# Scale row and biases of the experts made during the output product, their sum begun in the first expert, the router by halves of the tokens

## The chip, the cores and the metric

The kernel runs on one core of one Trainium2 chip. The metric is the device time of one execution in microseconds (us), the median of several runs. Times inside an execution are counted from the start of its span. Engine names are those of the profile: PE is the matrix engine (PEld its weight loads, PEq its sequencer), DVE the vector engine, ACT the scalar engine, POOL the GpSimd engine, SP the engine that issues most DMAs. A matmul in full float32 leaves two records in the trace, a transpose one.

## The reference, cut to what matters

The program is two blocks over 256 tokens of width 1024. The first has attention with an output product and then a mixture of 32 experts, of which each token uses 4; the second has an mLSTM layer and an attention layer with their dense feed-forward parts. The change lies where the first block goes from attention to the experts:

```
x = x + g_a * _merge(ya, yb, ga, gb, w_oa, w_ob, w_out)      # output product
hx = _modulate(_rmsnorm(x, norm_mlp), sh_m, sc_m)
logits = (h @ router_w + router_b).astype(jnp.float32)
top_logit, top_e = lax.top_k(logits, TOP_K)
top_w = jax.nn.softmax(top_logit, axis=-1)
...
gate = jnp.minimum(xe @ w_gate[e] + b_gate[e], SWIGLU_LIMIT)
up = jnp.clip(xe @ w_up[e] + b_up[e], -SWIGLU_LIMIT, SWIGLU_LIMIT)
act = (up + 1) * (gate * jax.nn.sigmoid(SWIGLU_ALPHA * gate))
return act @ w_down[e] + b_down[e]
...
x = x + g_m * moe(hx)
```

## The kernel before, in words

The five engines have programs of their own, written out by hand, which wait on semaphores; nothing reorders them. The 256 tokens are two halves q of 128 rows, the 1024 columns two halves h of 512.

*Output product.* Steps t = 42 to 49 each take one slice of 128 rows of `w_out`. ACT and DVE split each slice into a high and a low float32r part (`high_a`, `low_a`), and PE runs three matmuls per product (`mm3`, L625 to L627). Steps 42 to 45 run inside the loop over t; the last four slices run quarter by quarter (q, h), L876 to L888, so that the rows of one quarter are finished while PE is at the next. ACT works for step t + 4 in the pass of step t, in order.

*Norm and router.* `next_norm("a")` on DVE and ACT adds each quarter to X (two DVE operations), squares it (ACT, L1561), takes the root (ACT, L1566) and makes a diagonal matrix of the inverse. `turn_rows_a(q)` on PE (L805 to L812) multiplies X by it, which turns and scales 128 columns k at a time into PSUM banks 0 to 3; ACT evicts the even k (L1574), DVE the odd (L1861) into `b.h2`. `turn_rows_a(0)` runs before the last quarter of the product, `turn_rows_a(1)` after it. Then PE makes the router's logits for both halves (L381), spreads the row g_m over 128 partitions (8 matmuls, L900, banks 0 and 1), turns `b.h2` back to token rows (16 transposes, L909), turns the picks (L913, L915) and the places (L918, L919), and begins the experts' sum with weights times scaled down-biases (4 matmuls into the banks `b.Y`, L926). ACT, after its last eviction, loads the table of Exp (L1594), copies the spread row twice per half (`b.gm`, `b.gm2`), issues the four DMAs of the gate and up biases (`b.brow`, L1602), then computes the router's exponential for q = 0 (L1611), evicts turned tokens (`rows_to_gather`), the exponential for q = 1 and the rest. DVE does the router's steps for q = 0 and 1 (L2130 to L2142), scales the down-biases (`bdn`, L2145), counts the tokens of each expert (L2148 and on) and writes a flag.

*Experts.* Every engine loads the flag into a register and branches; with these inputs the branch for few tokens per expert is taken. For each expert PE gathers its tokens (L941, by the selection that DVE makes in `select`), turns them (L952), adds the biases (L985) and runs the gate and up products in two parts, k0 = 0 and k0 = 4 (L990, 32 records each). A part's end frees two of six slots of weights, each of 2 MB. In the middle come `put_back` of the expert before (L960, not in expert 0), `turn_act(ex, 0)`, the gather for the next expert and `turn_act(ex, 1)`, then the down product in two parts (L1023), each of which frees one slot. SP issues the loads in one fixed order and waits for the freed slot before each (L605); the first expert's six slots are loaded before the router.

## Time and profile before

| | |
|---|---|
| median of 3 runs | 1972.54 us (1970.38 to 1973.79) |
| profiled execution | 1973.61 us |
| its span | 1971.6 us, so 2.0 us lie around it |
| mean granted clock of PE | 0.972 of full |
| PE busy | 93% of the span |
| DMA, mean | 286 GB/s |

The profile's page names the costliest groups and the chain of work that ended last. The change touches some 60 us of the span between the end of the output product and the first expert, so the views that matter here are the chain, the timeline and the queue of SP in that stretch. PEclk is the share of the full clock of 2.4 GHz that PE was granted: 0.50 is 1.2 GHz.

### The profile page before, as it was taken

Reading aid. Unit: us, or ns where it says so; the run is one execution under the profiler, and the core shown is the slowest. Engines: PE = TensorE matmul, PEld = TensorE weight load, DVE = VectorE, ACT = ScalarE, POOL = GpSimd, SP = SyncE. Lnnn points to the kernel's source line nnn. Section 1 sums busy time; section 2 is a strip of 40 time slices with the busy share of each in tenths; the row PEclk is TensorE's granted clock in tenths of the full one; section 3 lists DMA queues with packets and bytes.
Section 4 is the critical chain, followed back from the end, with each engine's and each line's share of the span. In section 5 each row is a group of like instructions: output and inputs, shape, how many; then the busy total and the mean of one; then the engine's idle time right before and its main releaser. Section 6 shows DMA issues by size and latency. Waiting matters only on the chain.

```text
span 1971.6 us, 24815 instructions
## 1 busy us (share of the span) xinstructions
PE 1828.4 (93%) x10349; PEld 1126.6 (57%) x10349; DVE 772.6 (39%) x1348; ACT 601.0 (30%) x1076; POOL 19.5 (1%) x59
## 2 busy tenths in 40 slices
PE   5999988899999999999999999979999999899999
PEld 4987757233333333333333333348789997778998
DVE  2665534323222223223222222144555455645554
ACT  3456543111110111111110111145554445555442
POOL 0100010000000000000000000000000000000000
PEclk9999988899999999999999999989999999999999
DMA  8523764499999999999999999965326454324550
GB/s 294 195 74 124 258 258 175 187 427 429 426 427 428 428 427 428 428 426 429 426 429 426 429 426 428 427 225 207 122 95 212 171 202 161 128 86 159 184 178 36
DMA packets 122050, 563.27 MB, mean 286 GB/s; under 512 B 7216, under 2 KB 53424, under 8 KB 97360
## 3 DMA queue, kind: packets, MB, share of 16 engines
q1 hardware_dynamic: 120912, 558.44, 70.8%
q10 hardware_dynamic: 1024, 3.22, 0.4%
q8 instruction: 84, 1.38, 0.3%
q14 instruction: 30, 0.25, 0.0%
HBM read 560.58 MB, written 1.05 MB: 285 GB/s over the span
## 4 chain that ended last, share of the span: by engine, by line
PE 63%; DMA 29%; DVE 3%; ACT 2%; issue 1%; SPq 0%; ACTq 0%; DVEq 0%
DMA ring<-in_w_up 27%; PE ps L990 15%; PE ps L625 12%; PE ps L626 12%; PE ps L627 12%; PE ps L1023 3%; DMA ring<-in_w_ada 2%; PE ps L637 1%; PE ps L1114 1%; DVE part L1864 1%; PE ps L732 1%; PE ps L941 1%; ACT part L1347 1%; PE ps L960 1%; PE ps L742 1%
## 5 line engine op out<-in xcount | busy, mean ns | idle before, releaser
L625 PE MATMUL ps<-part,part 128*128 128x256 f32 (+2 forms) x1592 | 512.9, 322 | 10.9 <-DVE part L1864 8.6
L990 PE MATMUL ps<-ring,arena 128*64 128x512 f32 x2048 | 463.1, 606 | 46.1 <-DMA ring<-in_w_up 46.0
L626 PE MATMUL ps<-part,part 128*128 128x256 f32 (+2 forms) x1592 | 504.5, 317 | 0.0
L627 PE MATMUL ps<-part,part 128*128 128x256 f32 (+2 forms) x1592 | 503.8, 316 | 0.0
L1864 DVE TENSOR_TENSOR part<-ring,part 128x1024 fp32r<-128x1024 f32 (+1 forms) x299 | 313.2, 1090 | 136.9 <-ACT part L1347 136.3
L990 PEld LDWEIGHTS ps<-ring,arena 128*64 128x64 f32 x2048 | 157.5, 139 | 349.5 <-issue 349.5
L625 PEld LDWEIGHTS ps<-part,part 128*128 128x128 f32 (+1 forms) x1592 | 306.7, 193 | 42.4 <-issue 16.0
L627 PEld LDWEIGHTS ps<-part,part 128*128 128x128 f32 (+1 forms) x1592 | 306.0, 192 | 19.8
L626 PEld LDWEIGHTS ps<-part,part 128*128 128x128 f32 (+1 forms) x1592 | 306.8, 193 | 17.6
L1347 ACT ACTIVATE part<-ring 128x1024 fp32r<-128x1024 f32 (+1 forms) x299 | 271.8, 947 | 29.3 <-PE ps L627 24.1
L1861 DVE TENSOR_SCALAR arena<-ps 64x512 f32<-64x512 f32 x128 | 88.1, 688 | 400.4 <-PE ps L990 394.7
L1023 PE MATMUL ps<-ring,arena 128*64 128x512 f32 x1024 | 233.6, 598 | 0.0
L1657 ACT ACTIVATE arena<-arena 64x512 f32<-64x512 f32 x64 | 40.3, 630 | 633.8 <-DVE arena L1861 633.8
L1347 ACT ACTIVATE arena<-ps 128x256 f32<-128x256 f32 (+3 forms) x192 | 84.0, 476 | 240.1 <-PE ps L952 117.5
L1864 DVE TENSOR_TENSOR arena<-ps,arena 128x512 f32<-128x512 f32 x40 | 27.4, 686 | 302.5 <-PE ps L1023 295.8
L1023 PEld LDWEIGHTS ps<-ring,arena 128*64 128x64 f32 x1024 | 67.9, 136 | 117.6 <-issue 115.4
L1864 DVE TENSOR_TENSOR ring<-ps,ring 128x256 f32<-128x256 f32 (+1 forms) x52 | 23.8, 464 | 146.3 <-ACT ring L1771 145.8
L1771 ACT ACTIVATE ring<-ps 128x256 f32<-128x256 f32 x44 | 16.9, 384 | 185.4 <-PE ps L627 185.4
L1864 DVE TENSOR_TENSOR arena<-arena 64x512 f32<-64x512 f32 (+2 forms) x68 | 70.0, 1029 | 2.4
L1347 ACT ACTIVATE ring<-ps 128x512 f32<-128x512 f32 (+2 forms) x87 | 43.2, 518 | 72.6 <-PE ps L627 17.3
L960 PE MATMUL ps<-arena 64*128 64x512 f32 x256 | 63.6, 615 | 0.8 <-DVE arena L1864 0.8
L941 PE MATMUL ps<-arena 128*64 128x512 f32 x256 | 63.2, 615 | 0.0
(245 smaller groups left out, 1009.0 us busy)
## 6 DMA issues: line engine op xcount, KB each, us to landing
ring<-in_w_gate SPq DMA_DIRECT2D x64, 2048.0 KB, 16.8
ring<-in_w_up SPq DMA_DIRECT2D x64, 2048.0 KB, 21.4
ring<-in_w_down SPq DMA_DIRECT2D x64, 2048.0 KB, 19.0
ring<-in_ffn_w_in SPq DMA_DIRECT2D x44, 1024.0 KB, 7.8
ring<-in_w_ada SPq DMA_DIRECT2D x12, 2048.0 KB, 11.2
ring<-in_ffn_w_out SPq DMA_DIRECT2D x10, 2048.0 KB, 8.0
ring<-in_w_in SPq DMA_DIRECT2D x8, 2048.0 KB, 11.6
ring<-in_a_w_in SPq DMA_DIRECT2D x6, 2048.0 KB, 10.8
```

The lines of the kernel that those rows point to most:

```text
L625: e.matmul(out, x[0], y[0], start=first, stop=False, skip_group_check=True)
L626: e.matmul(out, x[0], y[1], start=False, stop=False, skip_group_check=True)
L627: return e.matmul(out, x[1], y[0], start=False, stop=last, skip_group_check=True)
L637: i = e.matmul(PS[bank][32 * g:32 * g + 32, :], a.c32[:, g + 4 * r, :], w[:, g + 4 * r, :], start=r == 0, stop=r == 1, skip_group_check=True)
L941: i = e.matmul(PS[p][CAP * h:CAP * h + CAP, :], S[:, CAP * q:CAP * q + CAP], b.htok[:, q, 512 * h:512 * h + 512], start=q == 0, stop=q == ...
L960: i = e.matmul(b.Y[q][h], b.PwT[ex % 2][CAP * h:CAP * h + CAP, 128 * q:128 * q + 128], b.yg[ex % 2][CAP * h:CAP * h + CAP, :], start=False ...
L990: i = e.matmul(PS[p + h][CAP * r:CAP * r + CAP, :], xg[:, k0 + k, :], W(("moe_" + "gu"[r], ex, k0))[:, k, 512 * h:512 * h + 512], start=False,
L1023: i = e.matmul(PS[p + 1][CAP * h:CAP * h + CAP, :], aT[:, k0 + k, :], W(w)[:, k, 512 * h:512 * h + 512], start=k0 == 0 and k == 0, stop=k0 ...
L1347: return e.activation(out, src, ACT.Copy)
L1657: e.activation(gus[:, 2, 512 * h:512 * h + 512], gus[:, 0, 512 * h:512 * h + 512], ACT.Sigmoid, scale=1.702).then_inc(*s_sig.up(ex, h))
L1861: return e.tensor_scalar(out, x, s1, s2, op0, op1) if op1 is not None else e.tensor_scalar(out, x, s1, None, op0)
L1864: return e.tensor_tensor(out, x, y, op)
```

## The change

Six edits, all in the stretch above:

1. The spread of g_m on PE moves from behind the logits to step t = 44 of the output product, into banks 2 and 3; ACT's four copies of it move to the same step, between `high_a(48)` and `high_a(49)`. PE waits for the last copy before the first of the four quarters.
2. DVE's two scalings of `bdn` move ahead of `next_norm("a")`.
3. The four DMAs of `b.brow` move from ACT to SP, behind the load of slab `gb1`, with a wait for the last heads' norm (`s_kn.of(9)`).
4. The logits of q = 0 are made between the product's end and `turn_rows_a(1)`, those of q = 1 after it.
5. ACT evicts all eight turned pieces of q = 1; DVE evicts none of them and can go on to the router of q = 0.
6. The four matmuls that begin the sum move into expert 0, behind its gate and up products (and to the head of the other branch, which does not run here).

`b.gm`, `b.gm2`, `b.xtok` and `b.brow` get other places in memory, since they are now written earlier.

```diff
@@ sync_program
+                if key == ("in", "gb1"):
+                    e.wait_ge(*s_kn.of(9))
+                    for r, n in enumerate(("b_gate", "b_up")):
+                        for h in range(2):
+                            at = 32 * (2 * r + h)
+                            e.dma_start(b.brow[at:at + 32, :], A[n][0][:, 512 * h:512 * h + 512]).then_inc(*s_brow.up(r, h))
@@ tensor_program
-                        e.wait_ge(*(s_ulo if i % 2 else s_uhi).of("moe", i - 4))
+                        e.wait_ge(*(s_ulo if i % 2 and i < 12 else s_uhi).of("moe", i - 4))
...
+                if t == 44:
+                    e.wait_ge(*s_mod.of(11))
+                    for h in range(2):
+                        for j in range(4):
+                            i = e.matmul(PS[2 + h][:, 128 * j:128 * j + 128], M(5, 4 * h + j).to_broadcast([128, 128]), C("ident"),
+                                         start=True, stop=True, skip_group_check=True)
+                        i.then_inc(*s_gm.up(h))
+            e.wait_ge(*s_gm2.of("half", 1))
...
-            turn_rows_a(1)
-            e.wait_ge(*s_small_ld.of("biases"))
-            e.wait_ge(*s_uhi.of("moe", 14))
-            e.wait_ge(*s_ulo.of("moe", 15))
-            for q in range(2):
+            def logits(q):
                 mm(e, PS[4 + q][:, 0:NE], [(b.h2[:, k, 128 * q:128 * q + 128], rw[:, k, :]) for k in range(KT)]
                    ).then_inc(*s_logit.up(q))
-            for h in range(2):
-                for j in range(4):
-                    i = e.matmul(PS[h][:, 128 * j:128 * j + 128], M(5, 4 * h + j).to_broadcast([128, 128]), C("ident"),
-                                 start=True, stop=True, skip_group_check=True)
-                i.then_inc(*s_gm.up(h))
+            e.wait_ge(*s_small_ld.of("biases"))
+            e.wait_ge(*s_uhi.of("moe", 6))
+            e.wait_ge(*s_ulo.of("moe", 7))
+            logits(0)
+            turn_rows_a(1)
+            e.wait_ge(*s_uhi.of("moe", 15))
+            logits(1)
...
                     if ex:
                         put_back(ex - 1)
+                    else:
+                        begin_sum()
                     turn_act(ex, 0)
@@ scalar_program
+                if t == 44:
+                    for h in range(2):
+                        e.wait_ge(*s_gm.of(h))
+                        copy(b.gm[:, 512 * h:512 * h + 512], PS[2 + h]).then_inc(*s_gm2.up(h))
+                        copy(b.gm2[64 * h:64 * h + 64, :], PS[2 + h][64 * h:64 * h + 64, :]).then_inc(*s_gm2.up("half", h))
...
-                    if stage == "a" and i % 2:
+                    if stage == "a" and q == 0 and i % 2:
@@ vector_program
-                    if stage == "a" and i % 2 == 0:
+                    if stage == "a" and (q or i % 2 == 0):
...
+            for h in range(2):
+                e.wait_ge(*s_gm2.of(h))
+                tt(bdn[:, 512 * h:512 * h + 512], bdn[:, 512 * h:512 * h + 512], b.gm[0:NE, 512 * h:512 * h + 512], ALU.mult
+                   ).then_inc(*s_bdn.up(h))
             next_norm("a")
```

`begin_sum` is the removed loop of L921 to L927 as a function, with the same waits and no signal.

PE from the last matmul of the product (L627, in the changed kernel L632) to the first gather (L941, now L954), before; L811 is `turn_rows_a(1)`, L381 the logits, L900 the spread, L909 the transposes of `b.h2`, L926 the begun sum:

```order
L811 MATMUL ps<-arena,X 128x128 [waits u_high,diag_ready]
...
L381 MATMUL ps<-rw,arena 128x32 [waits u_low,u_high,small_tables_loaded]
L381 MATMUL ps<-rw,arena 128x32 x15
L900 MATMUL ps<-con,mod 128x128 x8
L909 MATMUL ps<-con,arena 128x128 x8
...
L926 MATMUL ps<-bdn,arena 128x512 [waits h_turn_evicted,down_bias_scaled,picks_evicted]
L926 MATMUL ps<-bdn,arena 128x512 x3
L934 TENSOR_LOAD arena [waits places_evicted,bias_rows_loaded,flag_ready]
```

and in the changed kernel (L816 is `turn_rows_a(1)`, L918 the transposes of `b.h2`):

```order
L381 MATMUL ps<-rw,arena 128x32 [waits u_low,u_high,small_tables_loaded]
L381 MATMUL ps<-rw,arena 128x32 x7
L816 MATMUL ps<-arena,X 128x128 [waits u_high,diag_ready]
...
L816 MATMUL ps<-arena,X 128x128 [waits u_high] x4
L381 MATMUL ps<-rw,arena 128x32 [waits u_high]
L381 MATMUL ps<-rw,arena 128x32 x7
L918 MATMUL ps<-con,arena 128x128 x16
...
L947 TENSOR_LOAD arena [waits h_turn_evicted,places_evicted,bias_rows_loaded,flag_ready]
```

Half of the logits went ahead of the turning, the spread and the begun sum are gone from between the turning and the load of the flag (L934, now L947).

ACT behind its last squares of the norm, before; L1574 evicts turned pieces, L1347 is every copy, L1611 the exponential:

```order
L1574 ACTIVATE arena<-ps,mod,small 128x128 [waits u_turned] x4
L1594 ACT_TABLE_LOAD
L1347 ACTIVATE arena<-ps 128x512 [waits gain_row_spread]
L1347 ACTIVATE arena<-ps 64x512
L1347 ACTIVATE arena<-ps 128x512 [waits gain_row_spread]
L1347 ACTIVATE arena<-ps 64x512
L1602 DMA arena<-in_b_gate 32x512 x2
L1602 DMA arena<-in_b_up 32x512 x2
L1611 ACTIVATE small<-small 128x32 [waits router_steps]
```

and now, with L1595, L1363 and L1623 for the same:

```order
L1595 ACTIVATE arena<-ps,mod,small 128x128 [waits u_turned] x8
L1615 ACT_TABLE_LOAD
L1623 ACTIVATE small<-small 128x32 [waits router_steps]
L1363 ACTIVATE arena<-ps 128x512 [waits h_turned] x2
L1623 ACTIVATE small<-small 128x32 [waits router_steps]
```

Four copies and four DMA issues no longer stand before the first exponential, and four more evictions stand before the table load.

PE in expert 0 of the changed kernel: L1003 is the gate and up products, L937 the begun sum, L985 `turn_act`, L954 the gather for expert 1:

```order
L1003 MATMUL ps<-ring,arena 64x512 [waits slot5_loaded,slot3_loaded]
L1003 MATMUL ps<-ring,arena 64x512 x15
L937 MATMUL ps<-bdn,arena 128x512 [waits h_turn_evicted,down_bias_scaled,picks_evicted]
L937 MATMUL ps<-bdn,arena 128x512 x3
L985 MATMUL ps<-con,arena 128x64 [waits expert_act]
```

The begun sum now stands behind both parts of the gate and up products and ahead of all that follows.

## Rows read from the trace of the kernel before

**Rows 1.** Page, the chain that ended last: shares of the span by line.
```profile
DMA ring<-in_w_up 27%; PE ps L990 15%; PE ps L625 12%; PE ps L626 12%; PE ps L627 12%; PE ps L1023 3%; DMA ring<-in_w_ada 2%; PE ps L637 1%; PE ps L1114 1%; DVE part L1864 1%; PE ps L732 1%; PE ps L941 1%; ACT part L1347 1%; PE ps L960 1%; PE ps L742 1%
```
**Rows 2.** Window of 50 us: PE, PEld, DVE, ACT, POOL busy, PEclk, DMA share, GB/s.
```profile
414.00:464.00 50.00, 49.07 (x240) 16.79 (x238) 15.36 (x26) 5.50 (x11) 0.00 (x0) 1.00 1.00 426
```
**Rows 3.** Chain in order of time, 290 to 400 us: start, us, what.
```profile
303.09 0.87 PE ps L802 x8
...
324.26 0.24 PE ps L627
...
327.79 3.80 PE ps L811 x16
...
332.17 7.00 PE ps L381 x32
339.18 3.59 PE ps L900 x16
...
351.30 7.01 PE ps L926 x8
358.31 3.11 PE ps L941 x8
...
364.52 13.91 PE ps L990 x64
```
**Rows 4.** Queue of SP in order of time: start, us, what, loads.
```profile
191.02 0.58 SPq L605 DMA_DIRECT2D ring<-in_w_in  x1
204.80 0.37 SPq L605 DMA_DIRECT2D ring<-in_w_ada  x1
...
371.58 0.33 SPq L605 DMA_DIRECT2D ring<-in_w_gate  x1
...
398.05 0.33 SPq L605 DMA_DIRECT2D ring<-in_w_gate  x1
```
**Rows 5.** Windows of 1 us, same columns: the granted clock.
```profile
326.00:327.00 1.00, 0.00 (x0) 0.00 (x0) 0.16 (x1) 0.77 (x3) 0.00 (x0) 0.80 0.00 0
...
343.00:344.00 1.00, 1.00 (x8) 1.00 (x7) 0.00 (x0) 0.98 (x2) 0.00 (x0) 0.67 0.24 47
...
360.00:361.00 1.00, 1.00 (x6) 0.24 (x2) 0.00 (x0) 0.00 (x0) 0.00 (x0) 0.64 0.00 0
```
**Rows 6.** Timeline: start, us, engine, line, operation, [idle before, releaser].
```profile
307.89 1.23 DVE L1864 TENSOR_TENSOR part<-ring,part 128x1024 fp32r<-128x1024 f32 x1 [0.60 <-ACT part L1347]
...
328.63 0.46 ACT L1574 ACTIVATE arena<-ps,mod,small 128x128 f32<-128x128 f32 x1 [1.41 <-PE ps L811]
...
331.66 1.28 ACT L1594 ACT_TABLE_LOAD   x1
...
335.87 0.19 DVE L1864 TENSOR_TENSOR small<-ps,rb 128x32 f32<-128x32 f32 x1 [3.84 <-PE ps L381]
...
344.60 0.32 ACT L1611 ACTIVATE small<-small 128x32 f32<-128x32 f32 x1 [0.60 <-issue]
...
345.44 0.59 ACT L1347 ACTIVATE arena<-ps 128x512 f32<-128x512 f32 x1
345.62 0.18 DVE L1864 TENSOR_TENSOR small<-ps,rb 128x32 f32<-128x32 f32 x1
...
347.55 0.19 DVE L2140 SCALAR_TENSOR_TENSOR small<-small 128x32 f32<-128x32 f32 x1
```
**Rows 7.** Timeline from the picks to the first selection, same columns.
```profile
348.60 0.42 ACT L1347 ACTIVATE arena<-ps 32x128 f32<-32x128 f32 x2 [0.76 <-PE ps L915]
349.34 0.67 DVE L2148 TENSOR_TENSOR_SCAN arena<-arena 32x256 f32<-32x256 f32 x1
...
353.09 1.77 DVE L1861 TENSOR_SCALAR arena<-con,small 128x64 f32<-128x64 f32 x8 [1.05 <-issue]
```
**Rows 8.** Timeline of DVE behind the end of the experts' branch, same columns.
```profile
1307.13 0.23 DVE L1864 TENSOR_TENSOR part<-wgt,part 128x64 fp32r<-128x64 f32 x1 [4.85 <-issue]
```
**Rows 9.** Line L934, PE's load of the flag: ns min/median/max, first and last start us.
```profile
L934 PEldq TENSOR_LOAD <-arena x1: 492/492/492, 352.1 to 352.1; - x1
```

More of the change, by code:

```diff
@@ L403, in build @@
         b.yg, b.PwT = [alloc(512) for _ in range(2)], [alloc(T) for _ in range(2)]
-        b.S, b.xtok = [alloc(6 * CAP) for _ in range(2)], alloc(512)
-        assert at[0] >= mark + 10 * T + 4 * 512
-        b.gm, b.gm2 = alloc(D), alloc(512)
+        b.S = [alloc(6 * CAP) for _ in range(2)]
+        at[0] = mark + 10 * T + 4 * 512
         b.h3 = at[1][:, at[0]:at[0] + KT * T].rearrange("p (k n) -> p k n", k=KT)
         b.gus = [alloc3(3, D, CAP) for _ in range(2)]
+        b.brow = alloc(512)
         at[0] = mark
@@ L905, in tensor_program @@
                     n = 2 * q + g
-                    if q:
-                        e.wait_ge(*s_gm2.of("half", g))
                     for j in range(4):
@@ L1029, in tensor_program @@
             with e.Else():
+                begin_sum()
                 for n in range(4):
@@ L1594, in scalar_program @@
             e.preload_act_table(ACT.Exp)
-            for h in range(2):
-                e.wait_ge(*s_gm.of(h))
-                copy(b.gm[:, 512 * h:512 * h + 512], PS[h]).then_inc(*s_gm2.up(h))
-                copy(b.gm2[64 * h:64 * h + 64, :], PS[h][64 * h:64 * h + 64, :]).then_inc(*s_gm2.up("half", h))
-            for r, n in enumerate(("b_gate", "b_up")):
-                for h in range(2):
-                    at = 32 * (2 * r + h)
-                    e.dma_start(b.brow[at:at + 32, :], A[n][0][:, 512 * h:512 * h + 512]).then_inc(*s_brow.up(r, h))
             def rows_to_gather(n):
@@ L2116, in next_norm @@
                     turned_low(i)
+            e.wait_ge(*s_small_ld.of("biases"))
+            for h in range(2):
+                e.wait_ge(*s_gm2.of(h))
+                tt(bdn[:, 512 * h:512 * h + 512], bdn[:, 512 * h:512 * h + 512], b.gm[0:NE, 512 * h:512 * h + 512], ALU.mult
+                   ).then_inc(*s_bdn.up(h))
             next_norm("a")
-            e.wait_ge(*s_small_ld.of("biases"))
             def step(i, *key):
@@ L2142, in vector_program @@
                 ts(E, E, s[:, 3:4], None, ALU.mult).then_inc(*s_pick.up("W", q))
-            for h in range(2):
-                e.wait_ge(*s_gm2.of(h))
-                tt(bdn[:, 512 * h:512 * h + 512], bdn[:, 512 * h:512 * h + 512], b.gm[0:NE, 512 * h:512 * h + 512], ALU.mult
-                   ).then_inc(*s_bdn.up(h))
             e.wait_ge(*s_pickTe.of(1))
```

24 lines of the change are left out of this document (12 added, 12 removed).

## The prediction

> **What bounds the kernel now.** I read the chain that ended last first. Its largest single part is a transfer, the up weights of the experts, with 27% of the span [rows 1]: for most of the experts the chain runs through the weight stream, not through PE. The windows say the same: inside the expert loop the DMA share is 1.00 at 426 GB/s [rows 2]. So the question for any change ahead of the experts is when that stream starts. The queue of SP answers: the first load that needs a freed slot is issued at 371.58 [rows 4], when the first half of the first expert's gate and up products is done. Six loads of 2048 KB per expert are 12.6 MB, 29.5 us at 426 GB/s, and everything behind follows the start of this stream, as long as it never runs dry.
>
> Then I read the chain in order of time up to there. After the last product at 324.50 PE waits for the norm until 327.79, turns the second half (3.80), makes the logits (7.00), spreads the row (3.59), and after a stretch of small steps on DVE and ACT begins the sum (7.01), gathers (3.11) and starts the gate and up products at about 364.5 [rows 3]. The one-microsecond windows give the clock: it falls to 0.50, that is 1.2 GHz, during 326 to 327, with PE idle since 324.50; it comes back during 343, falls again before the begun sum, and comes back during 360 [rows 5]. So logits, spread, begun sum and most of the gather run at half speed. On ACT the first exponential starts at 344.60 [rows 6], though the logits of q = 0 were read by DVE at 335.87 [rows 6]: ACT stood behind the spread, its copies and four DMA issues.
>
> **The change part by part**, on the time axis of the profiled execution.
>
> *Spread at t = 44.* Eight matmuls are 16 records. At the full clock 8 records of this width take 0.87 [rows 3], so 16 take 1.75, where PE is saturated: the end of the product moves from 324.50 to 326.25. ACT's four copies take 0.6 each [rows 6], 2.4 in all; the first two lie beside the second half of the spread, and PE has another step of the product (12 matmuls of some 0.23, 2.7) before it waits for the last copy, so that wait is nothing. The last slice's split on DVE ended at 309.12 before [rows 6]; it now comes behind the copies, about 3 later, at 312.2, and PE reads it in the fourth product of the first quarter, near 313. That cover is 0.7; if it is gone the cost is what is missing. DVE's two scalings of the biases (0.6 each) fit between that and the first quarter's end, near 313.6. If all of this were late the whole chain would move by up to 1.
>
> *Bias rows on SP.* Behind `gb1`, issued at 191.02, SP has nothing to do until 204.80 [rows 4]: 13 us for four issues of 64 KB. The event it waits for belongs to a step long past. Cost 0; if the issues took longer than that gap, the load behind them would be late by the rest, and I allow 1.
>
> *Logits of q = 0.* They fall into the wait for the norm, 326.25 to 329.54 (both ends of the old wait, moved by 1.75). At full clock they take a quarter of the 7.00 [rows 3], 1.75; at half clock 3.5, which would push the turning by 0.2. Cost 0.
>
> *Turning and evicting q = 1.* First eviction at 328.63 [rows 6] + 1.75 = 330.38. PE at half clock gives a piece each 0.43 (ACT's fourth, the seventh piece, ended by the table load at 331.66 and so began by 331.2, six pieces behind 328.63), and an eviction on ACT takes 0.46 [rows 6], so the last ends at 330.38 + 3.0 + 0.46 = 333.85. ACT alone keeps up with PE at half clock. The table load of 1.28 [rows 6] follows, to 335.2, and the exponential of q = 0 to 335.5: it needs only DVE's steps, which began at 329.8.
>
> *Logits of q = 1.* Half clock: 3.50, 333.95 to 337.45; DVE reads them 0.2 later, 337.65.
>
> *Transposes of `b.h2`* at half clock, 0.22 a record as in the spread (3.59 / 16) [rows 3]: four groups end at 338.35, 339.25, 340.15, 341.05. ACT copies two groups (0.6 each), to 340.0, then does the exponential of q = 1 (0.32), 340.3. DVE's steps between the read of the logits and the sum took 345.62 to 347.55 [rows 6], 1.93, so DVE is there at 339.6 and waits 0.75 for ACT; from the sum to the weights 0.7, so 341.1. ACT meanwhile copies the other two groups, to 341.8, and the picks (2 x 0.42 [rows 7]), to 342.65. DVE's count starts at 342.75; before it started at 349.34 [rows 7], behind the scaling of the biases that is now gone from there.
>
> *To the first gather.* From that count to the end of the first selection: 349.34 to 353.09 plus half of 1.77 [rows 7], 4.63. The gather could start at 347.4. PE no longer has the begun sum (7.01) in front of it, but now waits out the selection. Before it started at 358.31 [rows 3]. Saved: 358.31 - 347.45 = 10.9.
>
> *The load of the flag on PE.* Before it began at 352.1 and took 0.49 [rows 9], hidden by the begun sum; now nothing hides it. DVE needs 1.05 for its own flag and branch [rows 7], and the selection comes on top of that, so I take 0 for PE, and the other end is the 4.85 that DVE idles behind the branch's end [rows 8]: then PE is ready at 345.3 + 4.85 = 350.2 and the start is 2.7 later. The Trainium skill, "Runtime: NRT & Kernel Launch", section "Instruction fetch mechanics", says that a taken branch to a target outside the prefetched window costs an instruction fetch. The row at the branch's end looks like it, the 1.05 at its entry does not. By that rule, were PE's entry such a branch, the sum would be 2.7 smaller.
>
> *Clock at the gather.* Before, the clock came back during 360, 2.4 us into the gather [rows 5]. Now PE has been nearly idle from 341.4 to 347.4, so it starts at 1.2 GHz again, with no begun sum ahead of it. I take 2 us more at half clock than before, 1.0 lost. The ends: 0, and 5.8 (the first rival below).
>
> *Begun sum in expert 0.* At full clock half of 7.01, 3.5, on PE between two parts of the same expert. It stands behind the release of 371.58. The next start of an expert's loads was at 398.05, the stream of the expert before it lasts to 371.58 + 29.5 = 401.1, both plus the same latency: a slack of 3.0. So 0.5 would come through; but the small steps behind it on PE wait for DVE and ACT, which run on beside it, and I expect that to give the half back. PE's round from release to release is 26.5 and the stream's 29.5, so the slack is whole again an expert later. Cost 0, other end 3.5.
>
> **Sum.** Stream start and all behind it: -10.9 + 1.0 = -9.9. The profiled execution took 1973.61, of which 1971.6 are its span, so 1963.7. The median of the runs shown is 1.07 lower, 1972.54, and the forecast for a median is 1962.6.
>
> **Rivals** (for a median).
>
> *The clock comes back late.* With neither a long transposing stretch nor the begun sum ahead, the half clock may last through the gather and the first half of the gate and up products. From 326.6 to 343.7 it lasted 17 us although PE was busy [rows 3, 5]; the second time it was back 9.4 us after the begun sum's start at 351.30. 14 us from the gather's start, against 2.4 before, lose (14 - 2.4) / 2 = 5.8 in place of 1.0: 1967.4. The chance is 20%.
>
> *The clock never falls in the router.* The logits of q = 0 fill more than half of the idle stretch in which it fell. Then logits and transposes take half: the last eviction ends at 333.3, the logits of q = 1 at 335.2, and ACT's chain ends with the picks at 339.3, so the gather starts at 344.0 and 14.3 are saved, 13.3 with the loss at the gather: 1959.2. Against it: the remaining gap of 1.5 us and thin work around it. 9%.
>
> *The begun sum starves the stream.* If PE is slower in expert 0 than I take, the slack of 3.0 is used up and up to 3.5 come back: 1966.1. The margin is nothing by my own sum. 13%.
>
> *PE's branch*, as above, 2.7 back: 1965.3. 4%.
>
> *Slower: the half clock holds through the whole first expert and into the second.* Every us of it costs 0.5 on PE once it decides. 45 us from the gather's start lose 22.5 - 1.2 for what was there before, less the slack of 3.0, 18.3, against 10.9 saved: +7.4, 1979.9. It turns slower where the half clock lasts more than about 30 us. Against it: the clock came back within the gather [rows 5], and the first expert's 64 records took 13.91, the full rate [rows 3]. 4%.
>
> **How the numbers follow.** The forecast as worked out has 50%. 1962.6 is its time. The cases reach from 1959.2 to 1967.4 and the executions before differed by some 3 us, so the range is 1957.5 to 1968. A difference under 0.2%, 3.9 us, can't be told from no change with this kernel. Faster by more than that means under 1968.6: the forecast, and nearly all of the other cases but the last, 0.90. Within 0.2%: the upper end of the late clock, 0.06. Slower: 0.04.
>
> **What would show it right or wrong.** Right: the last product near 326.3; logits in two groups of about 1.8 and 3.5; first exponential near 335; gather near 347.4; begun sum of some 3.5 in eight records behind the first expert's gate and up products; the first gate load of the second expert near 361.7, that of the third about 26.5 to 29.5 later with no gap in the DMA share. Wrong: a stream start later than 365, DMA share under 0.95 in the 30 us behind it, a PE wait between the spread and the first quarter, a clock of 0.50 under the gate and up products, or a weight load of the first block that is later than before behind the bias rows. The forecast fails most easily in the clock: two of its terms assume which level is granted.

## The result and the profile after

The changed kernel takes 1958.13 us (median of 4 runs, 1955.34 to 1960.53), against 1972.69 for the kernel before beside it: ratio 0.9925, 95% interval 0.9912 to 0.9937. The forecast was 1962.6, faster. The profiled execution took 1958.61, its span is 1956.8 and its mean granted clock 0.979. The nine runs of this kernel in two series (the second in the experiments below) have a median of 1958.61 and reach from 1955.34 to 1963.69.

Line numbers have moved: the product is now L630 to L632, the spread L885, the turning L816, the transposes L918, the picks L922 and L924, the gather L954, gate and up L1003, the begun sum L937, SP's loads L604. On the page the chain still has the up weights as its largest part [rows 1]:

```profile
DMA ring<-in_w_up 28%; PE ps L1003 14%; PE ps L630 12%; PE ps L631 12%; PE ps L632 12%; PE ps L1038 3%; DMA ring<-in_w_ada 2%; PE ps L642 1%; DVE part L1876 1%; PE ps L1130 1%; PE ps L954 1%; PE ps L737 1%; ACT part L1363 1%; PE ps L747 1%; PE ps L973 0%
```

The queue of SP shows both the gain and a loss (start, us, what, loads; answers to [rows 4]):

```profile
190.02 0.58 SPq L604 DMA_DIRECT2D ring<-in_w_in  x1
190.65 3.75 SPq L610 DMA_DIRECT2D arena<-in_b_gate  x2
194.44 0.89 SPq L610 DMA_DIRECT2D arena<-in_b_up  x2
203.80 0.38 SPq L604 DMA_DIRECT2D ring<-in_w_ada  x1
...
356.49 0.33 SPq L604 DMA_DIRECT2D ring<-in_w_gate  x1
...
388.86 0.33 SPq L604 DMA_DIRECT2D ring<-in_w_gate  x1
```

The stream of weights starts at 356.49, where it was 371.58: 15.09 earlier. But the next expert's loads start 32.37 later, not 26.47. One expert's weights last 29.5 by the prediction's estimate (29.36 from start to start where the stream bounds the loop), so the queues ran empty for some 2.9. The bias rows took 4.7 us of SP and the load behind them is 13.8 behind `gb1`'s, as before: they cost nothing. The load of `gb1` itself is 1.0 earlier than before, ahead of anything that the change touches: executions differ by that much before the change begins.

The chain in order of time (start, us, what; answers to [rows 3]):

```profile
305.35 1.78 PE ps L885 x16
...
324.89 0.24 PE ps L632
...
328.95 3.38 ACT arena L1595 x8
332.35 1.28 ACT L1615
333.64 0.33 ACT small L1623
...
337.65 0.43 ACT arena L1363 x2
338.11 0.69 DVE arena L2160
...
342.86 3.47 PE ps L954 x8
...
349.43 13.88 PE ps L1003 x64
363.31 4.03 PE ps L937 x8
367.96 3.61 PE ps L954 x8
```

The spread is in the chain with 1.78. ACT's evictions, the table load and the exponential of q = 0 follow each other without a gap, and behind the first expert's products now stands the begun sum. PE's own timeline (start, us, engine, line, operation, idle before, releaser) has what is off this chain:

```profile
324.96 1.86 PE L381 MATMUL ps<-rw,arena 128*128 128x32 f32 x16
328.43 3.41 PE L816 MATMUL ps<-arena,X 128*128 128x128 f32 x16 [1.60 <-DVE arena L1873]
332.38 1.97 PE L381 MATMUL ps<-rw,arena 128*128 128x32 f32 x16 [0.55 <-ACT arena L1595]
334.19 1.94 PE L918 MATMUL ps<-con,arena 128*128 128x128 f32 x16
```

The logits come in two groups, each 1.9 long; the transposes take 1.94. All three ran at the full clock, but the turning between them (3.41) didn't. The one-microsecond windows say when it was granted, the five-microsecond one what the DMA did behind the begun sum (start:end, length, PE, PEld, DVE, ACT, POOL busy, PEclk, DMA share, GB/s; answer to [rows 2, 5]):

```profile
328.00:329.00 1.00, 0.57 (x4) 0.57 (x5) 0.90 (x8) 0.05 (x1) 0.00 (x0) 0.93 0.00 0
332.00:333.00 1.00, 0.62 (x6) 0.62 (x6) 0.00 (x0) 0.98 (x2) 0.00 (x0) 0.86 0.00 0
...
345.00:346.00 1.00, 1.00 (x4) 0.00 (x0) 0.00 (x0) 0.00 (x0) 0.00 (x0) 0.54 0.00 0
366.00:367.00 1.00, 1.00 (x3) 0.11 (x1) 0.56 (x1) 0.00 (x0) 0.00 (x0) 0.70 1.07 459
373.00:374.00 1.00, 1.00 (x6) 0.29 (x6) 0.00 (x0) 0.23 (x1) 0.00 (x0) 0.88 1.11 475
381.00:386.00 5.00, 5.00 (x28) 1.49 (x22) 1.36 (x5) 0.00 (x0) 0.00 (x0) 1.00 0.91 338
```

The half clock lasts from 329 to 332 only, under the turning; then from 339 to 346 with the gather in it; and a third time from 366 to 373, from the end of the begun sum on. Before, it lasted from 326 to 343 and from 350 to 360, and none fell behind the first expert. From 381 the DMA moves 338 GB/s, where it is near 426 inside the loop [rows 2]: the dry stretch.

**The account.** The span is 14.8 shorter: -15.1 up to the stream's start, +2.65 between it and the last expert's second gate and up part (910.36 before, 913.01 now), -0.9 from there to the next block's turning and -1.5 behind that. The change doesn't touch the last two. From that part of the last expert to the end of the span the fourteen profiles take between 685.2 and 689.7, with the same work there; the kernel before is the longest of them (689.66, the changed one 687.30). The starts of that part on PE's timeline, before and after, show one piece of it:

```profile
1281.94 8.79 PE L990 MATMUL ps<-ring,arena 128*64 128x512 f32 x32 [2.38 <-DMA ring<-in_w_up]
```

```profile
1269.50 7.09 PE L1003 MATMUL ps<-ring,arena 128*64 128x512 f32 x32 [1.69 <-DMA ring<-in_w_up]
```

Before, the clock was at 0.50 from 1282 to 1286, and the same 32 records took 1.7 longer.

### The profile page after: what moved, and what is told of

Read it like the earlier page. It is cut to its first block, busy times and chain, and to the rows that moved or that the text cites. A ratio compares the mean times of both kernels' runs of the same rounds, so it can differ in the third digit from the quotient of the medians.

```text
span 1956.8 us, 24817 instructions
## 1 busy us (share of the span) xinstructions
PE 1814.3 (93%) x10349; PEld 1117.3 (57%) x10349; DVE 770.5 (39%) x1344; ACT 602.0 (31%) x1080; POOL 19.5 (1%) x59
## 4 chain that ended last, share of the span: by engine, by line
PE 62%; DMA 30%; DVE 3%; ACT 3%; issue 2%; SPq 0%; DVEq 0%; ACTq 0%
DMA ring<-in_w_up 28%; PE ps L1003 14%; PE ps L630 12%; PE ps L631 12%; PE ps L632 12%; PE ps L1038 3%; DMA ring<-in_w_ada 2%; PE ps L642 1%; DVE part L1876 1%; PE ps L1130 1%; PE ps L954 1%; PE ps L737 1%; ACT part L1363 1%; PE ps L747 1%; PE ps L973 0%
## 5 line engine op out<-in xcount | busy, mean ns | idle before, releaser
L630 PE MATMUL ps<-part,part 128*128 128x256 f32 (+2 forms) x1592 | 512.5, 322 | 10.9 <-DVE part L1876 8.6
L632 PE MATMUL ps<-part,part 128*128 128x256 f32 (+2 forms) x1592 | 503.4, 316 | 0.0
L1003 PE MATMUL ps<-ring,arena 128*64 128x512 f32 x2048 | 457.7, 600 | 46.4 <-DMA ring<-in_w_up 46.3
L1003 PEld LDWEIGHTS ps<-ring,arena 128*64 128x64 f32 x2048 | 156.1, 138 | 345.9 <-issue 345.9
L630 PEld LDWEIGHTS ps<-part,part 128*128 128x128 f32 (+1 forms) x1592 | 306.2, 192 | 42.4 <-issue 16.0
L632 PEld LDWEIGHTS ps<-part,part 128*128 128x128 f32 (+1 forms) x1592 | 305.7, 192 | 19.8
L1363 ACT ACTIVATE part<-ring 128x1024 fp32r<-128x1024 f32 (+1 forms) x299 | 271.8, 947 | 27.7 <-PE ps L632 22.1
L1363 ACT ACTIVATE arena<-ps 128x256 f32<-128x256 f32 (+3 forms) x192 | 84.0, 477 | 234.3 <-PE ps L965 117.7
L954 PE MATMUL ps<-arena 128*64 128x512 f32 x256 | 65.2, 632 | 2.8 <-DVE arena L1873 2.8
L1363 ACT ACTIVATE ring<-ps 128x512 f32<-128x512 f32 (+2 forms) x87 | 43.2, 518 | 71.9 <-PE ps L632 17.3
```

What stands on the lines that cost most here:

```text
L630: e.matmul(out, x[0], y[0], start=first, stop=False, skip_group_check=True)
L632: return e.matmul(out, x[1], y[0], start=False, stop=last, skip_group_check=True)
L954: i = e.matmul(PS[p][CAP * h:CAP * h + CAP, :], S[:, CAP * q:CAP * q + CAP], b.htok[:, q, 512 * h:512 * h + 512], start=q == 0, stop=q == ...
L1003: i = e.matmul(PS[p + h][CAP * r:CAP * r + CAP, :], xg[:, k0 + k, :], W(("moe_" + "gu"[r], ex, k0))[:, k, 512 * h:512 * h + 512], start=False,
L1363: return e.activation(out, src, ACT.Copy)
```

## The experiments

For each kernel I read the same moments. F is the end of the output product (read from PE's timeline, 0.15 below the chain's reading), G the start of the first gather, S the start of the stream (SP's first gate load for a freed slot), S2 that of the next expert, E the start of the last expert's second gate and up part.

| kernel | median us | ratio, 95% | F | G-F | S-G | S2-S | E-S |
|---|---|---|---|---|---|---|---|
| before | 1972.7 | 1 | 324.3 | 33.90 | 13.34 | 26.47 | 910.36 |
| changed | 1958.1 | 0.9925 [0.9912, 0.9937] | 325.0 | 17.89 | 13.63 | 32.37 | 913.01 |
| e0 changed, again | 1959.9 | 0.9944 [0.9930, 0.9957] | 326.0 | 18.00 | 14.02 | 30.93 | 911.20 |
| e1 sum before flag | 1962.4 | 0.9953 [0.9939, 0.9967] | 326.5 | 22.42 | 13.81 | 26.47 | 910.43 |
| e2 sum late | 1959.6 | 0.9939 [0.9925, 0.9952] | 324.7 | 18.09 | 13.92 | 26.47 | 910.41 |
| e3 only sum moved | 1970.5 | 0.9989 [0.9980, 0.9998] | 325.6 | 29.75 | 13.86 | 32.37 | 913.03 |
| e4 logits together | 1966.2 | 0.9964 [0.9950, 0.9978] | 325.1 | 24.42 | 14.19 | 30.88 | 911.15 |
| e5 spread behind logits | 1964.5 | 0.9956 [0.9939, 0.9972] | 325.0 | 22.91 | 13.74 | 32.38 | 913.06 |
| e6 bias rows on ACT | 1958.9 | 0.9936 [0.9919, 0.9952] | 326.0 | 18.06 | 13.95 | 30.94 | 911.49 |
| e7 dense filler | 1958.8 | 0.9935 [0.9920, 0.9950] | 325.1 | 17.96 | 13.55 | 29.30 | 910.90 |
| e8 evictions shared | 1960.6 | 0.9935 [0.9919, 0.9952] | 325.7 | 16.72 | 15.86 | 30.94 | 911.67 |
| e9 three together | 1958.6 | 0.9932 [0.9919, 0.9946] | 327.3 | 20.31 | 14.15 | 26.48 | 910.17 |
| e10 clock kept up | 1959.3 | 0.9935 [0.9922, 0.9949] | 328.7 | 22.64 | 12.13 | 26.48 | 910.29 |
| e11 filler cut | 1955.9 | 0.9910 [0.9894, 0.9927] | 325.8 | 17.90 | 12.12 | 26.48 | 910.31 |

The moments are from one profiled execution each, which need not be near the median: that of e4 is the fastest of its five, those of e9 and e10 the slowest of theirs. F alone varies by 4. The medians are of 4 to 11 runs and tell kernels apart from about 3 us upwards.

**e0_changed_again.** The changed kernel, unchanged.

> The changed kernel unaltered, timed beside the others on the same chip. Both theories: ratio to before 0.9925, between 0.991 and 0.994. Its profile tells in how many executions the clock falls under the begun sum.

Same G-F as in the first profile (18.00, 17.89), but 1.8 less between S and E. What differs there is the clock: at half for 3.4 behind the begun sum, for 6.8 in the first profile. More on it in e7.

**e1_sum_before_flag.** The begun sum back to its old place, all else as changed.

```diff
+            begin_sum()
             e.wait_ge(*s_flag.of())
...
-                    else:
-                        begin_sum()
```

> The changed kernel with the begun sum back ahead of the load of the flag. Theory A (the begun sum in expert 0 lets the weight stream run dry for 2.7 us and took 4.2 us from before the gather): the gather comes 4.2 us later than in the changed kernel, the stream has no gap, so 1.5 us slower than the changed kernel. Rival B (in expert 0 it costs nothing): 4.2 us slower.

```profile
342.00 7.03 PE L937 MATMUL ps<-bdn,arena 32*128 32x512 f32 x8
348.96 3.62 PE L955 MATMUL ps<-arena 128*64 128x512 f32 x8
```

On PE's timeline the sum runs at half clock, 7.03, and the gather stands right behind it: G-F is 4.4 longer, and nothing is dry any more (S2-S 26.47). So by the profiles moving the sum was worth some 2 to 4: it takes 4.4 off the path in front and returns 0.8 (e0) to 2.6 (first profile) behind. The medians differ by 2.5, which they can't tell from nothing by themselves; they don't contradict it.

**e2_sum_late.** The begun sum in experts 8 to 11, one matmul each; expert 0's `put_back` starts the banks.

```diff
-                                         b.yg[ex % 2][CAP * h:CAP * h + CAP, :], start=False, stop=ex == NE - 1,
+                                         b.yg[ex % 2][CAP * h:CAP * h + CAP, :], start=ex == 0, stop=ex == NE - 1,
...
+                    if 8 <= ex < 12:
+                        q, h = (ex - 8) // 2, (ex - 8) % 2
+                        e.matmul(b.Y[q][h], b.wT[:, 128 * q:128 * q + 128], bdn[:, 512 * h:512 * h + 512], start=False, stop=False,
+                                 skip_group_check=True)
```

> The changed kernel without any begun sum: the put-back of expert 0 starts the sum, and the four matmuls of weights times down-biases are added one each in experts 8 to 11, where PE waits 1.7 us for weights. Theory A: the stream has no gap, 2.7 us faster than the changed kernel. Rival B: the same time as the changed kernel, within 0.5 us.

```profile
356.69 0.33 SPq L604 DMA_DIRECT2D ring<-in_w_gate  x1
...
383.16 0.33 SPq L604 DMA_DIRECT2D ring<-in_w_gate  x1
```

SP's queue shows 26.47 between the two, and E-S is 910.41, the figure of before. The stream is never dry, and all the extra of the changed kernel between S and E is the begun sum. The medians (1959.6 and e0's 1959.9) can't tell the two apart, as against a profiled gain of 0.8 to 2.6.

**e3_only_sum_moved.** The kernel before with edit 6 alone, the same lines as in e1 the other way.

> The kernel before with the begun sum alone moved into expert 0. Theory A: the gather starts when the first selection is done, 4.2 us earlier than before, and the stream runs dry by up to 2.7 us: 1.5 to 4.2 us faster than before. Rival B: 4.2 us faster, no gap in the stream. Rival C (the clock comes back later without the begun sum ahead of the gather): no gain or up to 2 us slower than before.

G-F falls by 4.15, and 2.67 come back as a dry stream, which leaves 1.5. The measured gain is 2.2 (0.9989, 0.9980 to 0.9998): theory A. In the kernel before only 4.15 of the sum's 7.01 lay on the path, since the count and the selection ran beside it.

**e4_logits_together.** Both halves' logits behind the turning again; all else as changed.

```diff
-            logits(0)
             turn_rows_a(1)
             e.wait_ge(*s_uhi.of("moe", 15))
+            logits(0)
             logits(1)
```

> The changed kernel with the logits of both halves made behind the turning, none in the wait for the norm. From the product's end to the first gather the changed kernel takes 17.9 us. Theory C (the logits of q = 0 in that wait keep PE at 2.4 GHz through the turning): here the clock falls in the wait, turning and logits run at 1.2 GHz, and the stretch takes 22 us or more. Rival D (the clock is luck, the logits do not hold it): the clock under the turning is as in the changed kernel, and only the router's steps of q = 0 move behind the logits: 20.2 us.

```profile
328.71 3.75 PE L816 MATMUL ps<-arena,X 128*128 128x128 f32 x16 [3.51 <-DVE arena L1873]
333.01 7.04 PE L381 MATMUL ps<-rw,arena 128*128 128x32 f32 x32 [0.55 <-ACT arena L1595]
339.86 3.65 PE L918 MATMUL ps<-con,arena 128*128 128x128 f32 x16
```

PE idles 3.51 ahead of the turning, the clock falls in that wait and stays at half until 344: logits 7.04, transposes 3.65. G-F is 6.5 longer, the median 6 to 8. Moving 1.9 us of work can't do that by its own length. The clock adds 3.2 to the two groups of logits and 1.7 to the transposes; with the 1.9 that is 6.8, against 6.5 in G-F. The three profiles without logits in that wait (before, e3, e4) have the clock fall there, at 326 to 328, and stay at half for 17. In none of the eleven with them did it fall in that wait, of which 1.6 are left.

**e5_spread_behind_logits.** Edits 1 and 2 undone: the spread, its copies and the scalings where they were.

```diff
-                if t == 44:
...
             logits(1)
+            for h in range(2):
+                for j in range(4):
+                    i = e.matmul(PS[h][:, 128 * j:128 * j + 128], M(5, 4 * h + j).to_broadcast([128, 128]), C("ident"),
+                                 start=True, stop=True, skip_group_check=True)
...
```

> The changed kernel with the spread of the scale row, its copies and the scaling of the down-biases back behind the logits. The product ends 1.8 us earlier. Theory A': the first exponential waits for spread (1.8 to 3.6) and four copies, and the scaling (1.2) stands before the count again: the stretch to the gather takes 22 to 25 us, and the kernel is 2.5 to 5 us slower than the changed one. Rival B' (ACT and DVE had room there): the stretch stays under 20 us and the kernel is within 0.5 us of the changed one.

```profile
331.91 1.97 PE L381 MATMUL ps<-rw,arena 128*128 128x32 f32 x16 [0.91 <-ACT arena L1589]
333.71 3.41 PE L908 MATMUL ps<-con,mod 128*128 128x128 f32 x16
```

G-F is 4.9 longer: the spread at mostly half clock (3.41), and ACT's copies ahead of its first exponential, against the spread inside the product, which makes that longer by 2.0: from the turning behind step 43 (303.56 in e5, 301.58 in the changed kernel) to F it takes 21.4 here and in the other two kernels without the spread there, 23.4 with it. F is no earlier than in the changed kernel only because this execution was 2.0 behind already at 303.56. So edits 1 and 2 are worth 2.9 in the profiles. The median is 4.6 to 6.4 longer.

**e6_bias_rows_on_act.** Edit 3 undone: ACT issues the four DMAs, behind its table load.

```diff
             e.preload_act_table(ACT.Exp)
+            for r, n in enumerate(("b_gate", "b_up")):
+                for h in range(2):
+                    at = 32 * (2 * r + h)
+                    e.dma_start(b.brow[at:at + 32, :], A[n][0][:, 512 * h:512 * h + 512]).then_inc(*s_brow.up(r, h))
```

> The changed kernel with the four DMAs of the bias rows issued by ACT again, behind its table load. Theory A': four issues of 0.44 us stand before the first exponential, which comes 1.8 us later; the stretch to the gather grows by 1.4 us. Rival B': issues run beside ACT's work, since the exponential is not what ends the wait; the stretch stays at 17.9 us, within 0.3.

```profile
332.91 1.28 ACT L1609 ACT_TABLE_LOAD   x1
332.92 0.92 ACTq L1613 DMA_DIRECT2D arena<-in_b_up  x2
334.20 0.32 ACT L1621 ACTIVATE small<-small 128x32 f32<-128x32 f32 x1
```

The issues run on ACT's queue beside its last evictions and the table load, and the exponential follows the table at once. The edit is worth nothing that shows: G-F 18.06, median 1958.9 against 1959.9 and 1958.1.

**e7_dense_filler.** As e2, and in expert 0, where the begun sum stood, four matmuls of 128 rows whose result is overwritten: extra work.

```diff
+                    else:
+                        for q in range(2):
+                            for h in range(2):
+                                e.matmul(b.Y[q][h], b.htok[:, 0, 128 * q:128 * q + 128], b.htok[:, 1, 512 * h:512 * h + 512], start=True,
+                                         stop=False, skip_group_check=True)
```

> The begun sum is made late, in experts 8 to 11, as in e2_sum_late; in its place in expert 0 stand four dense matmuls (128 rows by 512 columns, full float32, 8 records) into the same banks, whose result is overwritten. They are extra work and change no output. In the changed kernel the clock fell to 0.50 while the begun sum, whose matmuls have 32 rows, ran in the first expert, and the stream of weights ran dry by 2.7. Theory F: the clock fell because the 32-row matmuls are thin; with 128 rows in the same place it stays near full, the filler takes 1.8 to 2.2 for 8 records, and the next expert's loads start 28 to 30 behind the first's: no gap in the stream, median within 1 of e2_sum_late. Rival F': the clock falls at this place whatever the matmuls are (the pause behind the first expert's products is its cause): the filler takes 3.4 to 4.0, the loads are 31 to 32.4 apart, the stream is dry for 1.5 to 2.9, median 1.5 to 3 above e2_sum_late.

PE's timeline first of e0, then of e7:

```profile
364.80 3.70 PE L937 MATMUL ps<-bdn,arena 32*128 32x512 f32 x8
368.82 3.31 PE L954 MATMUL ps<-arena 128*64 128x512 f32 x8
```

```profile
363.37 3.70 PE L1032 MATMUL ps<-arena 128*128 128x512 f32 x8
...
367.39 1.94 PE L954 MATMUL ps<-arena 128*64 128x512 f32 x8
```

Both groups of 8 records take 3.70. Behind the 32-row ones the gather of the next expert takes 3.31, behind the 128-row ones 1.94: there the clock stayed at 1.00 throughout, S2-S is 29.30 and E-S 910.90. The begun sum stands in expert 0 in seven profiles, and in every one the clock falls during it or within 1 us of its end: for 3.4 us in e0, e4, e6 and e8 (S2-S near 30.9), for 6.8 in the changed kernel, e3 and e5 (32.4). In e1, e2, e7, e9, e10 and e11 it does not fall there. So theory F holds as far as one filler in one profile can show. My figure for 8 records at full clock, 1.8 to 2.2, was wrong by my own rows: they are 3.5 to 3.7. Priced by E-S: the length alone 0.5, with 3.4 us of half clock 0.8 to 1.3, with 6.8 us 2.65. The four kernels with S2-S near 30.9 differ by 0.5 themselves, so the first figure is no more than that scatter.

**e8_evictions_shared.** Edit 5 undone: DVE evicts the odd pieces of q = 1 again.

```diff
-                    if stage == "a" and q == 0 and i % 2:
+                    if stage == "a" and i % 2:
...
-                    if stage == "a" and (q or i % 2 == 0):
+                    if stage == "a" and i % 2 == 0:
```

> The changed kernel with the evictions of q = 1 shared by ACT and DVE again. Theory E (with the clock at 2.4 GHz PE gives a piece each 0.22 us and ACT's 0.42 per eviction is what bounds the turning): the last eviction comes 1.5 to 2 us earlier, and the stretch to the gather takes about 1.2 us less than in the changed kernel. Rival F (DVE's router steps of q = 0, now late, cost as much as is won): the same or up to 1 us more.

```profile
329.17 2.19 PE L816 MATMUL ps<-arena,X 128*128 128x128 f32 x16 [1.60 <-DVE arena L1874]
...
342.44 3.68 PE L955 MATMUL ps<-arena 128*64 128x512 f32 x8 [2.78 <-DVE arena L1874]
...
348.62 1.98 PE L999 MATMUL ps<-arena,con 32*64 32x512 f32 x8 [0.69 <-ACT arena L1364]
```

The gather comes 1.2 sooner behind F, for at full clock PE's turning takes 2.19 where it doesn't wait for ACT, and eight evictions on ACT alone take 2.90 (e0; 3.38 in the first profile, where the turning was at half clock). But here the half clock lasted from 338 to 351 (the biases took 1.98 in place of 1.09) and S-G is 2.2 longer. From F to S it is 32.6, against 31.5 in the first profile and 32.0 in e0: no gain. Whether edit 5 costs anything in the median stays open.

**e9_three_together.** e2 and e8 together, and the table of Exp loaded while ACT waits for the turning.

```diff
                 root_of(1)
+                if stage == "a":
+                    e.preload_act_table(ACT.Exp)
                 for i in range(8, 16):
...
-            e.preload_act_table(ACT.Exp)
```

> Three things at once on the changed kernel: the begun sum is spread over experts 8 to 11 (as e2_sum_late), DVE takes its share of the evictions of q = 1 again (as e8_evictions_shared), and ACT loads the table of Exp between its second root and these evictions, where it waits 1.1 for PE, not behind them. Expected by adding up: the stream is not dry (-2.7 in the profile), the last product to the first gather is 16.7 as in e8, and the exponential of q = 0 comes 1.28 earlier. Theory H: the path to the gather goes through the logits and the router of q = 1 by then, so the earlier table gives at most 0.4: gather 16.3 to 16.7 behind the last product, stream start 13.9 to 15.9 behind the gather by the clock; profiled span 1953 to 1956, median 1956 to 1958.5. Rival H': the path still goes through ACT's exponential of q = 0: the gather comes 1 to 1.3 earlier still, 15.4 to 15.7. A second rival: the table load takes the wait of 1.1 and 0.2 more, the first evictions are late and nothing is gained: 16.9 or more.

No number for the gather held in the profile: G-F was 20.31. On PE's timeline the clock had fallen already at 321, in the wait ahead of the product's last quarter, was back from 326 to 332, and was at half again to 342:

```profile
323.70 0.77 PE L630 MATMUL ps<-part,part 128*128 128x512 f32 x1
...
334.61 3.59 PE L381 MATMUL ps<-rw,arena 128*128 128x32 f32 x16 [0.59 <-DVE arena L1880]
338.01 3.65 PE L919 MATMUL ps<-con,arena 128*128 128x128 f32 x16
```

Up to the wait for the turning this kernel's work on every engine is e8's, so the fall at 321 is the clock's course in one execution, and not the edits. The median of five runs is 1958.6, just above what the parts sum up to. The early table shows no gain here or in e11, whose G-F is that of the changed kernel. But in both the clock was at half under the turning, and in e8 it wasn't, so what it is worth stays open; it was not tried alone.

**e10_clock_kept_up.** As e9, with dense matmuls into a free bank where PE waits for the gather: extra work.

```diff
+            def keep_busy(m):
+                for j in range(m):
+                    e.matmul(PS[5], b.h2[:, j, 0:128], b.h2[:, 2 * (j % 4):2 * (j % 4) + 2, :], start=True, stop=True,
+            keep_busy(3)
             e.wait_ge(*s_pick.of("pos"))
...
+            keep_busy(2)
...
             e.wait_ge(*s_flag.of())
...
+                keep_busy(3)
                 gather(0)
```

> As e9_three_together, with eight dense matmuls (128 rows by 512 columns, 0.43 each at full clock) into a free bank where PE waits before the first gather: three before the places are turned, two before the flag's load, three between it and the gather. They are extra work and change no output. Theory G: the clock is at half when the gather starts because PE idles in front of it; with the filler it stays at 1.00 from 337 on, the gather takes 1.8 to 2.2 in place of 3.5 to 3.7, and the stream starts 12 to 12.6 behind the gather in place of 13.6 to 15.9: span and median 1 to 2.5 below e9_three_together. Rival G': the filler does not reach (its stretches are broken by the waits) and delays the turned places or the flag by 0.4 to 1.3 each: stream start as late as in e9_three_together or up to 2 later.

```profile
346.38 0.31 PE L934 MATMUL ps<-con,arena 32*128 32x32 f32 x2
...
346.65 4.73 PE L928 MATMUL ps<-arena 128*128 128x512 f32 x10
351.31 1.94 PE L962 MATMUL ps<-arena 128*64 128x512 f32 x8
```

Both answers at once. The clock is 1.00 from 344 on, the gather takes 1.94 and S-G is 12.13, 2.0 less than in e9. But between the turned places and the gather PE is never idle, and the gather is 4.9 behind them where it was 3.1: the filler behind the branch stands in its way. The expectation had each filler matmul at 0.43; it takes 0.95 (ten records, so five matmuls, in 4.73): 0.43 to 0.47 is one record. The filler was twice as long as planned. No gain in the median.

**e11_filler_cut.** As e10 with two matmuls at the first place, two at the second and none behind the branch.

> As e10_clock_kept_up with four dense matmuls in place of eight: two before the places are turned, two between these and the load of the flag, none behind the branch. In e10_clock_kept_up the gather ran at 1.00 (1.94 for its 8 records), but it started 4.78 behind the start of the turned places, where it was 2.96 in e9_three_together: the filler had eaten the gain. Theory G continued: without the three behind the branch the gather follows the places by 2.9 to 3.1 again; if the four suffice to keep the clock, the gather takes 1.9 to 2.2 and the stream starts 12.1 to 12.6 behind it, so from the turned places to the stream 15.1 to 15.7, against 17.1 in e9_three_together and in the changed kernel, and 16.9 in e10_clock_kept_up. Median 1955 to 1958. Rival: four are too few, PE idles some 2 in front of the gather, the clock is at 0.50 there, and the stream starts 13.6 to 15.9 behind the gather: median as e9_three_together, 1957.5 to 1960.

```profile
338.39 1.88 PE L928 MATMUL ps<-arena 128*128 128x512 f32 x4
340.54 0.31 PE L934 MATMUL ps<-con,arena 32*128 32x32 f32 x2 [0.27 <-DVE arena L1887]
...
340.81 1.98 PE L928 MATMUL ps<-arena 128*128 128x512 f32 x4
343.65 1.94 PE L962 MATMUL ps<-arena 128*64 128x512 f32 x8 [0.86 <-DVE arena L1887]
```

Now PE waits 0.27 and 0.86 between the groups, the clock is 1.00 from 333 on, the gather is 3.1 behind the turned places and takes 1.94. From the places to the stream it is 15.23, against 16.88 in the changed kernel and 17.26 in e9. The median is 1955.94, its runs within 1.4 of each other, the ratio 0.9910 (0.9894 to 0.9927). This is the fastest version of the study: below e0's interval (0.9930 to 0.9957), overlapping the first series' (0.9912 to 0.9937). That it beats the kernel before, by some 18 us, is shown. That it beats the changed one is likely but not shown: the two were never timed side by side, one of the two series of the changed kernel overlaps, and the kernel before was itself 1.5 slower beside e11 (1974.17) than beside the others. By the medians as they stand e11 is 2.2 to 4.0 lower.

## Why the prediction was right, and where it was not

The frame was as forecast: everything behind the stream's start follows it, the start moved because the gather moved, and the sign and the range held. Up to the gather, though, it was not the main case that came true but the second rival, the one with 9%, and behind it a good part of the third. The median came 4.5 below the forecast, on the side of that second rival's 1959.2. By the prediction's own steps:

**Product end and spread.** 325.13 for 326.25. The spread's records take 1.78 in the chain, predicted 1.75, and it moved the end by 2.0 (see e5). PE didn't wait for ACT's copies or the last slice's split: on DVE it ended by 310.8, before the 312.2 that I had put. The missing 1.1 is the head start of this execution and not the change: it was 1.35 ahead of the one before at the turning behind step 43 (301.58 for 302.93), in front of the spread.

**Logits of q = 0 in the wait.** Cost 0, right. What the forecast gave only the second rival's 9% is what they did besides: the clock did not fall in that wait. It fell later, at 329, and was back during 332. The rows of before show logits and transposes at half clock [rows 3, 5], and I carried that level over to a program in which the pause that went before it was more than half filled.

**Last eviction, logits of q = 1, picks.** The last eviction ended at 332.3 for 333.85, and ACT alone just kept up (3.38 for eight). The logits took 1.8 where 3.5 was put, the transposes 1.94 where it was 3.6. The picks' copies ended at 338.1 for 342.65. This is the main mis-sized term: 3.5 of the 4.6 are left when the product's end is taken out. The second rival's own times, less the 1.1 of the product's end, fit throughout: last eviction 332.2 for 332.3 measured, end of the logits 334.1 for 334.3, picks 338.2 for 338.1, gather 342.9 for 342.86. Its condition did not hold in full, as the clock was at half under the turning; that cost 0.5 on ACT (3.38 for the eight evictions, 2.90 in e0). e4 confirms the cause: with the logits out of the wait the transposes and logits are at half clock again, and G-F is 24.42, longer even than the 21.2 that was forecast.

**Count to gather.** 4.75 for 4.63, right; PE's branch cost nothing (gather 342.86, directly behind the selection's first part). DVE's idle time at the far end of the branch, which had made that rival [rows 8], says nothing of its entry. The rule of the Trainium skill, "Runtime: NRT & Kernel Launch", section "Instruction fetch mechanics", that a taken branch to a target outside the prefetched window costs an instruction fetch, would fit the far end here too, where DVE issued nothing for 5.68 in the changed kernel, though no run tells it from another cause; for PE's entry no run shows it.

**Clock at the gather.** It was at 0.50 until 345.9 as forecast, but S-G is 13.63 against 13.34 before, so 0.3 was lost, not 1.0: from the gather's start it lasted 3.1, against 2.4 before, where 2 more were put. The late clock, the rival with 20%, came near only in e8: half clock for 9.4 from the gather's start where that rival had 14, at a cost of 2.2. e10 and e11 size the whole term: at full clock S-G is 12.1, so the half clock here costs 1.2 to 2.1, and 3.7 in e8.

**Begun sum.** Put at 0, with 3.5 as its other end: it cost 2.65 in the first profile and 0.8 in e0. The slack of 3.0 holds at full clock as far as e7 can tell (0.5 for the same length, within the scatter), but the step took the clock for granted. The third rival (13%, up to 3.5 back) had the size and left its reason open; that the sum itself pulls the clock down was in no case of mine, though in the kernel before the clock had fallen at 350, ahead of the sum, and stayed at half beneath all of it.

**The sum.** To the gather -15.4 for -10.9 (of the difference 1.1 is the product's end, 3.5 the clock in the router); to the stream -15.1 for -9.9; begun sum +2.65 for 0; behind it -2.4 by chance; -14.8 for -9.9 in all. Two errors of the same kind, the clock in front and behind, with opposite signs. They cancel in part: -3.5 and -0.7 in front, +2.65 behind. Of the 5.1 by which the profile lies below its forecast of 1963.7, 3.5 are the head start and the end of the program, which the change doesn't touch. So the sign is earned, and the range held because it was drawn round the rivals; that the sum came as near as it did is partly luck.

**Parts of the gain.** By undoing one each, against e0: logits in the wait 6.4 of G-F, spread and scalings 4.9 less the 2.0 by which the product is longer, begun sum 4.4 less what the dry stream takes back, bias rows 0; the evictions on ACT alone lose 1.3 up to the gather. They can't be added, since several share the clock.

## What to carry to other kernels

In these kernels a wait of PE cost its own length and what ran at half clock behind it: 1.9 us of logits moved into a wait of 3.5 were worth 6. Before moving a thin matmul into full work, ask what it does to the clock there, and when two groups are compared in a trace, look at the granted clock of each first. When the stream of weights bounds the loop, only its start and its dry stretches count, so put what is movable where PE waits for the stream (experts 8 to 11 in e2, at no cost), not in the first expert.

## What the runs showed of the hardware

- Matmuls of 32 rows (32x512) took as long as those of 128 rows (8 records 3.70 each), but during them or within 1 us of their end, in the first expert, the granted clock went to 0.50 in 7 of 7 profiles; behind the 128-row ones it didn't, in the one that had them.
- The course of the clock is not fixed by the program: in kernels that differ little up to that point it fell behind the product anywhere from 329 to 338, and in e1, e9 and e10 once more at 321 to 323, ahead of the product's last quarter, which made the stretch from there to F 1.6 longer (5.3 to 5.4 for 3.8).
- ACT's DMA issues went beside its evictions and table load (332.08 to 333.84) without moving them.
- A table load took 1.28 in every profile, and Identity evictions ran on the table of Exp as on that of the root: 0.46 each either way (e9 to e11).
